# First weight unit in four transfers, last store on ScalarE's queue, and the gather's last columns on both sides of expert 1's first half

## The reference

```python
def reference(x, p, ...):
    h = x
    for i in range(2):
        hn = rms_norm(h, norm_mix[i])
        if i % 2 == 0:
            mix = even_mixer(hn, pos, even_w_in[j], ...)   # proj = hn @ w_in, the first product of the kernel
        else:
            mix = odd_mixer(hn, pos, odd_w_qkv[j], ...)
        h = h + mix
        h = h + hierarchical_moe(rms_norm(h, norm_ffn[i]), ...)
        gate = jax.nn.sigmoid(rms_norm(h, norm_ple[i]) @ ple_w_gate[i])
        h = h + gate * (p[i] @ ple_w_proj[i])
    return rms_norm(h, final_norm)

def hierarchical_moe(t, ...):          # 4 groups x 4 experts, d_ff 512
    ...                                # gates: softmax over groups, top 2 of 4 experts, softmax of these
    for gi in range(4):
        hg = jnp.einsum('td,edf->tef', t, w_gate[gi])
        hu = jnp.einsum('td,edf->tef', t, w_up[gi])
        act = jax.nn.silu(hg) * hu * gates[:, gi, :, None]
        out = out + jnp.einsum('tef,efd->td', act, w_down[gi])
```

## Time and profile before

| | |
|---|---|
| median of three runs | 768.54 us |
| profiled execution, its own time | 768.63 us |
| its span, first to last instruction | 766.4 us |
| TensorE busy | 735.6 us, 96% of the span |
| LDWEIGHTS busy | 342.8 us, 45% |
| VectorE, ScalarE, GpSimd busy | 273.5, 140.7 and 27.0 us |
| mean rate of the DMA engines | 322 GB/s |
| chain that ended last | PE 68%, DMA 15%, SyncE's queue 9%, issue 3%, DVE 2%, ACT 1% |

### The profile page before, as it was taken

The page is one execution under the profiler, slowest core; times in us unless marked ns, Lnnn a source line. Parts: engine busy times, 40 slices in busy tenths (PEclk is TensorE's granted clock), DMA queues, the critical chain, the costliest instruction groups (busy, mean ns, idle before and its releaser), DMA issues.

```text
span 766.4 us, 8322 instructions
## 1 busy us (share of the span) xinstructions
PE 735.6 (96%) x3178; PEld 342.8 (45%) x3178; DVE 273.5 (36%) x654; ACT 140.7 (18%) x347; POOL 27.0 (4%) x49
## 2 busy tenths in 40 slices
PE   8999999999999999889999999999999999988996
PEld 5445565664333333233445554484333333323444
DVE  1213341354326323223222464263435423322323
ACT  3000231321111111110221144232111111110131
POOL 2400000000000000000000000000000000000000
PEclk9999999999999999999999999999999999999998
DMA  9997241949999999999999690238999999999911
GB/s 345 318 347 286 107 165 59 422 179 404 421 419 422 421 419 422 421 421 419 385 293 287 260 370 6 80 141 318 422 420 423 421 420 421 422 420 422 402 70 55
DMA packets 49192, 246.67 MB, mean 322 GB/s; under 512 B 4520, under 2 KB 5640, under 8 KB 24576
## 3 DMA queue, kind: packets, MB, share of 16 engines
q1 hardware_dynamic: 46928, 241.03, 79.7%
q0 software_dynamic: 2048, 5.07, 2.0%
q10 hardware_dynamic: 176, 0.02, 0.0%
HBM read 245.04 MB, written 2.63 MB: 323 GB/s over the span
## 4 chain that ended last, share of the span: by engine, by line
PE 68%; DMA 15%; SPq 9%; issue 3%; DVE 2%; ACT 1%; POOLq 0%; POOL 0%; DVEq 0%; ACTq 0%
PE bank L618 27%; PE bank L872 17%; SPq L416 9%; PE bank L889 8%; DMA weights<-in_moe_w_up_dram 7%; DMA weights<-in_moe_w_down_dram 7%; PE bank L902 2%; PE bank L849 2%; PE bank L1040 1%; PE bank L602 1%; DMA residual<-in_x_dram 1%; PE bank L881 1%; PE bank L657 1%; PE bank L677 1%; PE bank L1098 1%
## 5 line engine op out<-in xcount | busy, mean ns | idle before, releaser
L872 PE MATMUL bank<-weights,expert_rows 128*64 128x512 f32 x1024 | 227.9, 594 | 14.1 <-DMA weights<-in_moe_w_up_dram 14.1
L618 PE MATMUL bank<-weights,normalised 128*128 128x512 f32 (+1 forms) x528 | 226.1, 582 | 2.7 <-DMA weights<-in_even_w_in_dram 1.2
L618 PEld LDWEIGHTS bank<-weights,normalised 128*128 128x128 f32 x528 | 98.1, 190 | 111.7 <-issue 109.4
L872 PEld LDWEIGHTS bank<-weights,expert_rows 128*64 128x64 f32 x1024 | 75.2, 137 | 158.0 <-issue 157.3
L889 PE MATMUL bank<-weights,hidden_turned 128*64 128x512 f32 x256 | 58.8, 598 | 1.3 <-DVE hidden_turned L1753 0.6
L889 PE MATMUL bank<-weights,hidden_turned_odd 128*64 128x512 f32 x256 | 58.8, 598 | 0.5 <-DMA weights<-in_moe_w_down_dram 0.5
L1339 ACT ACTIVATE gate_tanh<-bank 128x256 f32<-128x256 f32 x32 | 12.4, 386 | 199.1 <-PE bank L872 199.1
L1783 DVE TENSOR_TENSOR gather_onehots<-bank,expert_outputs 128x512 fp32r<-128x512 f32 x32 | 22.1, 692 | 55.4 <-ACT expert_outputs L1209 55.2
L1209 ACT ACTIVATE expert_outputs<-bank 128x512 fp32r<-128x512 f32 x32 | 19.1, 597 | 123.7 <-PE bank L889 123.7
L1753 DVE COPY hidden_turned<-bank 128x256 f32<-128x256 f32 x16 | 6.8, 424 | 84.6 <-PE bank L881 84.6
L1753 DVE COPY hidden_turned_odd<-bank 128x256 f32<-128x256 f32 x16 | 6.8, 425 | 81.1 <-PE bank L881 81.1
(11 more groups left out here) (249 smaller groups left out, 598.0 us busy)
## 6 DMA issues: line engine op xcount, KB each, us to landing
weights<-in_moe_w_gate_dram SPq DMA_DIRECT2D x64, 1024.0 KB, 18.5
weights<-in_moe_w_up_dram SPq DMA_DIRECT2D x64, 1024.0 KB, 20.6
weights<-in_moe_w_down_dram SPq DMA_DIRECT2D x64, 1024.0 KB, 22.6
weights<-in_even_w_in_dram SPq DMA_DIRECT2D x5, 2048.0 KB, 29.4
weights<-in_ple_w_gate_dram SPq DMA_DIRECT2D x4, 2048.0 KB, 30.9
weights<-in_even_w_out_dram SPq DMA_DIRECT2D x2, 2048.0 KB, 19.4
weights<-in_odd_w_qkv_dram SPq DMA_DIRECT2D x2, 2048.0 KB, 20.7
weights<-in_odd_w_out_dram SPq DMA_DIRECT2D x4, 1024.0 KB, 22.2
```

The costliest lines, as they stand in the source:

```text
L618: mm = pe.matmul(B[bank][:, 0:width], XT[:, k, tok(t)], w[:, k, :], start=(k == 0), stop=(k == KD - 1))
L872: mm = pe.matmul(bank[j * BLK:(j + 1) * BLK, :].rearrange("p (m f) -> p m f", m=2), rows[:, k, :], W[:, slots, a:a + FF // 2], start=(k == ...
```

## The change

Three places are edited; the rest of the diff renames semaphores.

1. Unit `U_IN` comes in four transfers of 512 KB (two k blocks each) with a semaphore each, in place of two of 1 MB, and token tile 1 of `x` is issued between the second and the third, in place of behind both. TensorE waits for each quarter by itself, and for the first two needs only VectorE's half of the transpose. Of the four products of zeros two are left.
2. In the experts, `gathered(1, 1)` is cut in two: its k = 4 and 5 stay ahead of `first_rows(1)`, its k = 6 and 7 go behind it. `spread()` is cut in two as well: the slot numbers go ahead of `other_rows(0)`, into bank 2 in place of bank 6, and the gates stay behind it.
3. The last store is issued by ScalarE, behind the instruction that makes its data.

```diff
@@ SyncE, start
-            for half in range(2):
-                sp.dma_start(unit(U_IN).rearrange("p (k n) -> p k n", k=KD)[:, 4 * half:4 * half + 4, :],
+            for quarter in range(4):
+                if quarter == 2:
+                    sp.dma_start(H[:, 1, :], x[0, P:SEQ, :]).then_inc(sem("x1_landed"), 16)
+                sp.dma_start(unit(U_IN).rearrange("p (k n) -> p k n", k=KD)[:, 2 * quarter:2 * quarter + 2, :],
                              even_w_in[0][:, order[0]:order[0] + 512].rearrange("(p k) n -> p k n", p=P)
-                             [:, 4 * half:4 * half + 4, :]).then_inc((landed(U_IN)[0], sem("first_unit_rest"))[half], 16)
-            sp.dma_start(H[:, 1, :], x[0, P:SEQ, :]).then_inc(sem("x1_landed"), 16)
+                             [:, 2 * quarter:2 * quarter + 2, :]).then_inc(first_unit_landed(quarter), 16)
@@ TensorE, start
+            def first_quarter(quarter):
+
+                pe.wait_ge(first_unit_landed(quarter), 16)
+                w = unit(U_IN).rearrange("p (k n) -> p k n", k=KD)
+                for k in range(2 * quarter, 2 * quarter + 2):
+                    mm = pe.matmul(B[0][:, :], XT[:, k, tok(0)], w[:, k, :], start=(k == 0), stop=(k == KD - 1))
+                return mm
...
             transposes(0, 0, (4, 5))
-            unread_zeros(4)
-            xt_ready(0, 0)
-            project_part(U_IN, 0, 0, 0, "in_ready")
+            unread_zeros(2)
+            pe.wait_ge(sem("xT_by_dve"), 1)
+            first_quarter(0)
+            first_quarter(1)
             transposes(0, 1, (6, 7))
-            project_part(U_IN, 0, 0, 1, "in_ready")
+            pe.wait_ge(sem("xT_by_act"), 1)
+            first_quarter(2)
+            first_quarter(3).then_inc(sem("in_ready"), 1)
             xt_ready(0, 1)
@@ TensorE, experts
+                def spread_slots():
+
+                    pe.wait_ge(sem("rows_by_act"), 4 * l + 2)
+                    for c in range(4):
+                        pe.matmul(B[2][:, tok(c)], RT[:, 404 + c:405 + c].to_broadcast([P, P]), ident, start=True, stop=True)
...
                 first_rows(0)
-                gathered(1, 1)
+                gathered(1, 1, (0, 1))
                 first_rows(1)
+                gathered(1, 1, (2, 3))
+                spread_slots()
                 other_rows(0)
-                spread()
+                spread_gates()
                 other_rows(1)
@@ ScalarE
-                copy(SROW.rearrange("p c s -> p (c s)"), B[6][:, :])
+                copy(SROW.rearrange("p c s -> p (c s)"), B[2][:, :])
...
             act.activation(OUTB[:, 1, 0:512], OUTB[:, 1, 0:512], ACT.Copy, scale=rstd(6, 1)).then_inc(sem("out_by_act"), 1)
+            act.wait_ge(sem("out_by_act"), 1)
+            act.dma_start(out[0, tok(1), 0:512], OUTB[:, 1, 0:512]).then_inc(sem("stored"), 16)
@@ SyncE, end
-            sp.wait_ge(sem("out_by_act"), 1)
-            sp.dma_start(out[0, tok(1), 0:512], OUTB[:, 1, 0:512]).then_inc(sem("stored"), 16)
             sp.wait_ge(sem("stored"), 48)
```

23 lines of the change are left out of this document (10 added, 13 removed).

## The result

The change makes the kernel slower. Its median is 774.4 us (20 runs, from 770.1); the kernel before has 770.8 in the same comparison (20 runs, from 768.1). The ratio is 1.0046, with a 95% interval from 1.0029 to 1.0064, or about 3.5 us. Forecast were 765.3 and a range of 763.4 to 767.6: the sign is wrong and the range misses.

The account below looks back on a forecast made before the run. TensorE, busy 96% of the span, was taken to bound the kernel up to about mid-experts in each layer, then the weight stream. 768.6 - 2.2 (start) - 1.0 (experts) - 0.1 (store) = 765.3 us, range 763.4 to 767.6.

Parts of the forecast that it names:

- The stream, a gain: Experts' weight stream: next transfer issued 1.13 us earlier wins back 0.6 and 0.9; after the new wait, 0.5 per layer.
- TensorE's slack: Second part of each layer's experts: the stream sets the time, TensorE has some 7 us spare, absorbing its own 0.45.
- the prediction's rule: Expert stream: a transfer lands at the later of pace, 2.5 us per MB, and issue plus 5.1 to 5.2.
- The bound given: Experts' part, loss side: -0.4 us per layer if the whole 1.35 wait at expert 0's second half is uncovered.
- What is late next: Start: second unit has 2.8 us of slack, no later wait before the experts tied to transfers; 2.2 us arrive whole.
- the start is absorbed: Rival: something not moving with TensorE, GpSimd's small loads or second or third unit, ends last; 767.5 us, chance 0.08.
- The clock: Half-clock stretch in layer 1's routing, 0.8 us on the path: may stay, go or appear in layer 0; counted nothing.
- Part 3: Last store issued by ScalarE at the kernel's end: 0.1 us won, bounds 0.9 lost and 0.7 won.
- Pieces cost: Rival at the start: each of two extra pieces delays what follows by about 0.5 us; 766.1 us, chance 0.10.
- The gather's wait is uncovered: Rival at expert 0's second half: slots' products give no cover, wait 1.35 us per layer; 767.1 us, chance 0.08.
- The slower rival: Expert stream: instruction fetches hold up DMA engines, up to 1.5 us each; a fourth more makes it 770; chance 0.05.

Follow-up runs that it names:

- slots_only: Kernel before with only the slots' spread moved ahead of expert 0's second half, gather whole: 771.96 us, ratio 1.0041.
- slots_wide: Kernel before with router products over 128 columns and the slots' spread ahead of expert 0's second half: 770.38 us, ratio 1.0002.
- start_only: Kernel before with only the first unit in four transfers and the new order at the start: 771.76 us, ratio 1.0036.
- start_small_loads_late: As start_only, but GpSimd issues its relative-bias copy and small loads only once the third unit has landed: 769.35 us, ratio 0.9978.
- change_loads_wide: Changed kernel with GpSimd's loads held until the third unit has landed and router products over 128 columns: 769.78 us, ratio 0.9986.
- start_loads_wide_store: As start_loads_wide, with the last store on ScalarE's queue as well: 766.48 us, ratio 0.9950.
- start_loads_wide: Kernel before with the start's edit, GpSimd's loads behind the third unit and router products over 128 columns: 766.19 us, ratio 0.9942.
- wide_logits: Kernel before with one edit, router products over 128 columns in place of 20: 767.60 us, ratio 0.9960.
- start_only_again: Same edit of the kernel before as start_only, run again on the second group's chip: 771.25 us, ratio 0.9999.
- start_four_zeros: As start_only, but with the four products of zeros of the kernel before in place of two: 770.56 us, ratio 0.9994.

## Why the prediction was wrong

**Part 2, "The stream, a gain", is the step that failed: 1.0 us won was forecast, 3.3 lost is measured.** It failed in two ways.

First, it computed two releases behind the moved instructions and left out the one between them. Expert 0's second half releases an up transfer and a down transfer. The prediction gave that half its new wait, right to 0.1 (0.56 and 0.54), then followed only what stands behind the next half (181.20), and took the lateness out of "TensorE's slack". But ahead of expert 0's second half now stand the slots' products and the wait; counted from the restart its release goes from 9.3 to 11.25 us. The lead of 4.2 that kept this transfer at pace falls to 2.7 in the mean (2.8 and 2.2 in the changed kernel's profile). That TensorE has slack is true and beside the point: the stream has none, and the stream is fed by TensorE's ends. slots_only and slots_wide show this release alone: everything else as before, lead 4.2 to 2.9, gap 2.48 to 3.5. They are 0.7 behind at the tenth landing and 1.4 at the end of the stream; what comes behind the tenth is mostly single gaps beside a fetch.

Second, the gain at expert 1's first half never came. By the prediction's rule, landing at the later of pace and issue plus 5.15, a lead above 2.7 loses nothing. The lead did rise from 1.8 to 2.7, and the gap rose too, from 3.3 to 3.8, where 2.5 was forecast. With leads of 2.2 to 3.0 the gaps run from 2.5 to 4.8. The rule held at a lead of 1.8 (3.3 forecast, 3.3 measured) and at 4.2, and was used at 2.7, where no row of before stood: the nearest are two with a lead of 3.6, one at pace (534.50) and one 1.5 behind it (181.20). There it was a guess at a price and should have been told as one, with an end on the loss side. The bound given, -0.4 per layer, covered only the uncovered wait. The prediction put the 1.5 at 181.20 down to an instruction fetch, and the packet beside it bears that out; it is no sign of a short lead. The waits for up weights, forecast at 12 us, are 16.1.

**The start, "What is late next", failed as well.** The forecast of the first 16 us was right in start_only (6.14 for 6.2, 14.00 for 14.1). Wrong was the sentence that nothing else ahead of the experts is tied to a transfer. It checked the second unit, and for the rest relied on waits of the kernel before, which only shows that there was none with the old distances. The third unit landed at 31.3, needed at 36.9. In the four profiles with the new start and the loads not held back it is needed at 34.8 to 36.4 and lands at 36.1 to 37.5; the six with the old start have 31.3 to 35.1. The rival "the start is absorbed" named the third unit, and it did end last. It also names GpSimd's small loads as something that stays put; they moved, since they follow token tile 1's norm, and that made it worse. In start_only 0.5 of 2.2 was left at the restart in the fastest run. Holding the loads back gave 1.4. That these loads hold up the third unit is shown by start_small_loads_late: 18.2 to landing in place of 29.7. How much of the 2.2 there is to win hangs on the first eight transposes. In the four profiles with the loads held these took 1.04, 1.60, 1.86 and 1.91 us, the second tile began 2.3, 1.5, 1.4 and 1.1 earlier than before, and the restart came 2.3, 1.5, 1.4 and 1.2 earlier (change_loads_wide, start_loads_wide_store, start_small_loads_late, start_loads_wide). So what is won arrives whole. In the kernel before the wait for the first unit hides this: with transposes of 1.91 in wide_logits the second tile still begins at 16.3. Why the transposes differ between profiles is not shown. With wide products, part 1 with the loads held back wins 1.4 in the medians too, across two groups (767.60 and 766.19).

**The clock was counted at nothing, with 0.8 to either side.** It is the largest part of the spread of the kernel before, and worth 3.1 us of its median in wide_logits. In the changed kernel's profile it took 0.8 more than before in layer 0 and 1.6 more between the layers. Whether part 1 makes it worse is not settled: the median time at half clock was 15.4 against 7.7 in the first group, but in the second 13.1 (start_only_again) and 13.8 (start_four_zeros, start_small_loads_late) against 13.8. At 38.76 in one profile it follows the new wait; that is one case. It can't be the cause of part 2's loss, since the steady pairs have that without it.

**Part 3 was small, as forecast, but not a gain.** Forecast 0.1 won, measured 0.07 lost from the last expert landing to the end (0.3 in the medians, which can't be told from none). The sum went by the spacing of the landings of before, 0.65; issued together the two stores land within 0.2 of each other, so they share the engines and do not queue one behind the other. The Trainium skill, "DMA: Bandwidth & Descriptors" (Issuing engines are not separate DMA queues), says that transfers started by different engines run on the same 16 DMA engines and interleave. The runs agree: the 0.4 that the issue was earlier did not reach the last landing (763.80 against 763.60).

The rivals: "Pieces cost" fell, with no wait between the quarters in any of the eight profiles of the new start; in six of them the quarters landed within the prediction's limits, in the changed kernel and start_loads_wide up to 0.7 later. The fixed cost per transfer that the Trainium skill gives ("DMA: Bandwidth & Descriptors", Anatomy of one DMA) is measured there for transfers that GpSimd issues, and these are SyncE's; by it, an estimate, Q3 would have come some 4 us later, and no profile shows that. "The gather's wait is uncovered" fell too: the wait is 0.56 and 0.54 in place of 1.35. The slower rival had the sign right and the mechanism in small part. At the release that the change makes late, no stretch of a changed order has a fetch beside the landing. But from the tenth landing to the end the change falls another 0.4 behind per layer, and the late landings there stand beside fetches.

Put together from the pairs that can be told apart: part 2 +3.3, part 1 between -0.5 and +2.4 by how the clock fell, part 3 about 0. The measured +3.5 lies in that. It is not split further, since the medians of whole runs carry the clock.

**What stays open.** Why GpSimd's copy, issued 1.6 us earlier in the changed kernel but 7 us behind the third unit's issue as before, moves that unit's landing from 31.3 to 35.1 (old start) to 36.1 to 37.5. Why a stream that is fed just in time loses up to 2.3 us, with the DMA engines busy 0.90 to 0.94 of the time and moving 334 to 356 GB/s. In the second window the busy share is 7 to 9% under that of the old order and the rate 17 to 18%, so engines stand empty and packets are slower as well; which brings the other is not shown. Why the two halves of part 2 cost 1.4 and 1.3 per layer and together 2.3. And why a fetch makes one landing late and leaves most others at pace: that the late ones stand beside fetches is counted here, and no run has moved a fetch.

## What to carry to other kernels

Where one queue is fed by the ends of another engine's work, list every release behind a moved instruction, each with its issue, its forerunner's landing and the lead between them, and trust "at pace" only for leads that a row shows at pace (here 3.9 us and more; at 2.0 to 3.1 it lost 0.2 to 2.3 us in 24 of 25 cases). Before a late landing is put down to its lead, look for an instruction fetch beside it.
When the start of a kernel gets earlier, list what the other queues issue by the same condition, and check each later transfer's landing against its new due time, with its own landing moved too.
Before medians are read, compare the time at half clock per run; if it differs, steady it first. Here widening eight narrow products per token tile did that at no cost and was worth more than the change was meant to win.

## What the runs showed of the hardware

- A stream that is fed just in time is slower than its pace even where each transfer is issued in time by its own length: 1 MB alone takes about 5.1 us from issue to landing, by which a lead of 2.7 would be enough, but at leads of 2.0 to 3.1 gaps of up to 4.8 were measured where 2.48 is the pace.
- Small loads and a copy from DRAM to DRAM on GpSimd's queue stretched a 2 MB transfer of SyncE's queue. It took 18.0 to 18.6 us to landing in the four profiles with them held back, 22.4 to 26.3 in the six with the old start, and 28.6 to 31.1 in the four with the new start.
- Router products over 128 columns in place of 20 took no time that shows (gather at 156.43 against 156.47) and kept the clock at 1.00 where it had been 0.50.
- Pieces of 512 KB queued behind each other landed 1.3 to 1.5 us apart in the eight profiles of the new start (last two quarters; 11.2 and 12.5 in the changed kernel). The first two, at the head of the queue, landed 1.8 to 3.0 apart. Both halves together were as fast as the whole 1 MB in most profiles (7.4 to 8.5 against 7.6 to 8.0), so no fixed cost per piece showed.
- 1 MB transfers with an instruction fetch of 16 or 8 KB beside them landed up to 1.5 us late, in the middle of a full stream as well; all 13 gaps over 2.8 us from the tenth landing on have such a packet beside them.
- One stretch of 3.4 us at half clock in the routing cost 0.8 us on the path, and 6.8 us in one piece cost 2.4.
